# Retention layers of a four-layer decoder: value and gate columns as seven block products, queries and keys as eight

## The reference

```python
def retention_mixer(x, s0, pos, w_in, norm_g, w_out):
    q, k, v, g = jnp.split(x @ w_in, [hk, 2 * hk, 2 * hk + hv], axis=-1)   # 1024, 1024, 2048, 2048 columns
    q = rope(q.reshape(b, l, RET_HEADS, RET_KEY_DIM), pos)
    k = rope(k.reshape(b, l, RET_HEADS, RET_KEY_DIM), pos) * (RET_KEY_DIM ** -0.5)
    o, s_fin = retention_chunked(q, k, v, s0)                              # 4 heads, chunks of 128 rows
    o = layer_norm_without_gain(o) * norm_g
    y = (jax.nn.silu(g) * o) @ w_out
    return y, s_fin
# every layer: x <- LN(alpha*x + mixer(x)); x <- LN(alpha*x + (silu(x @ a) * (x @ u)) @ w_out)
```

## Time and profile before

| | |
|---|---|
| median of three runs | 3132.41 us (3131.67 to 3133.89) |
| the profiled execution | 3135.14 us, span of its profile 3133.5 us |
| TensorE busy | 2976.5 us, 95% of the span |
| VectorE busy | 2024.7 us, 65% |
| ScalarE busy | 1248.3 us, 40% |
| granted clock, mean over the span | 0.971 of full speed |
| first retention layer, one head in the steady part (193.2 to 321.9 us) | 128.7 us |

### The profile page before, as it was taken

How to read it: one execution, slowest core, us unless ns; L and a number is a source line. 1 busy time by engine, 2 the same in 40 slices (tenths; PEclk the granted TensorE clock), 3 DMA queues, 4 the chain that set the end, 5 groups by cost and what they waited for, 6 DMA issues and landing times.

```text
span 3133.5 us, 54106 instructions
## 1 busy us (share of the span) xinstructions
PE 2976.5 (95%) x22655; PEld 2798.6 (89%) x22655; DVE 2024.7 (65%) x3062; ACT 1248.3 (40%) x1881; POOL 209.2 (7%) x342
## 2 busy tenths in 40 slices
PE   7999998999996999998898899999999999899998
PEld 7898996899996999987798799999989989699998
DVE  4555554868577957767886485857555555585766
ACT  3332332535343634443343153534523333253543
POOL 0102111000000000011011100000021110100000
PEclk9999999999997999998998999999999999899999
DMA  6344443233331333332122323333343433323332
GB/s 154 128 126 158 128 138 115 79 102 103 95 88 41 87 96 101 97 97 59 48 75 87 123 68 102 102 95 101 96 157 120 157 129 112 128 75 99 105 99 63
DMA packets 492948, 323.77 MB, mean 103 GB/s; under 512 B 29723, under 2 KB 469275, under 8 KB 492698
## 3 DMA queue, kind: packets, MB, share of 16 engines
q1 hardware_dynamic: 465906, 230.14, 26.3%
q0 software_dynamic: 26800, 90.18, 8.2%
HBM read 275.90 MB, written 44.82 MB: 102 GB/s over the span
## 4 chain that ended last, share of the span: by engine, by line
PE 88%; DVE 6%; ACT 3%; issue 2%; DMA 0%; POOL 0%; DVEq 0%; SPq 0%; ACTq 0%; POOLq 0%
PE ps L522 46%; PE ps L2728 8%; PE ps L2730 8%; PE ps L2729 8%; PE ps L572 2%; PE ps L2223 2%; PE ps L573 2%; PE ps L574 2%; PE ps L553 2%; PE ps L2355 2%; PE ps L2345 1%; DVE wf L2137 1%; ACT w_h L493 1%; DVE wf L2185 1%; PE ps L2820 1%
## 5 line engine op out<-in xcount | busy, mean ns | idle before, releaser
L522 PE MATMUL ps<-rr,w_h 128*128 128x260 f32 x3968 | 638.4, 283 | 2.2 <-DVE w_l L499 1.1
L499 DVE TENSOR_TENSOR w_l<-w_raw,w_h 128x1024 fp32r<-128x1024 f32 (+2 forms) x312 | 336.7, 1079 | 391.8 <-ACT w_h L493 390.6
L522 PEld LDWEIGHTS ps<-rr,w_h 128*128 128x128 f32 x3968 | 544.0, 189 | 4.1 <-issue 3.0
L493 ACT ACTIVATE w_h<-w_raw 128x1024 fp32r<-128x1024 f32 (+2 forms) x312 | 293.4, 941 | 481.0 <-PE ps L522 443.4
L522 PE MATMUL ps<-x_h,w_h 128*128 128x260 f32 x2016 | 419.7, 290 | 9.0 <-DVE w_l L499 7.5
L522 PE MATMUL ps<-x_h,w_l 128*128 128x260 f32 x2016 | 407.9, 284 | 0.0
L522 PE MATMUL ps<-x_l,w_h 128*128 128x260 f32 x2016 | 407.7, 284 | 0.0
L522 PE MATMUL ps<-rr,w_l 128*128 128x260 f32 x1984 | 400.2, 283 | 0.0
L2728 PE MATMUL ps<-x_h,w_h 128*128 128x260 f32 x1280 | 362.5, 283 | 5.7 <-ACT wf L1229 5.7
L2729 PE MATMUL ps<-x_l,w_h 128*128 128x260 f32 x1280 | 361.5, 282 | 0.0
L2730 PE MATMUL ps<-x_h,w_l 128*128 128x260 f32 x1280 | 361.0, 282 | 0.0
(11 more groups left out here) (330 smaller groups left out, 5070.6 us busy)
## 6 DMA issues: line engine op xcount, KB each, us to landing
w_raw<-in_ffn_w_in SPq DMA_DIRECT2D x176, 512.0 KB, 4.1
w_raw<-in_ret_w_in SPq DMA_DIRECT2D x96, 512.0 KB, 3.9
out<-wf POOLq DMA_DIRECT2D x72, 512.0 KB, 3.3
wf<-in_state_ret POOLq DMA_DIRECT2D x64, 512.0 KB, 5.6
w_raw<-in_ffn_w_out SPq DMA_DIRECT2D x64, 512.0 KB, 4.3
w_raw<-in_ret_w_out SPq DMA_DIRECT2D x64, 256.0 KB, 2.8
w_raw<-in_dsa_w_in SPq DMA_DIRECT2D x27, 512.0 KB, 3.9
w_raw<-in_ffn_w_out SPq DMA_DIRECT2D x32, 384.0 KB, 4.0
```

Source lines behind the costliest of these rows:

```text
L493: C.activation(whole(stage, k, half_of(w_h, n)[:, 0:m]), landed(stage, k, n, m), ACT.Copy).then_inc(S["w_hi"], 1)
L499: V.tensor_tensor(whole(stage, k, half_of(w_l, n)[:, 0:m]), landed(stage, k, n, m), whole(stage, k, half_of(w_h, n)[:, 0:m].bitcast(F32)), ...
L522: mm = M.matmul(ps[:, 2 * (n % 2) + b, 0:HALF], lhs[:, c, :], rhs[:, c, cols], start=(c == 0 and term == 0), stop=(c == cs - 1 and term == 2))
```

## The change

1. **Values and gates.** The units (4,5), (6,7), (8,9), (10,11) of each head become pairs. A pair is two units by all 520 rows, cut into blocks of four chunks and 260 rows, and formed as seven products instead of eight: P1, P2, P5, P6, P7, P4, P3, of 12 matmuls each, 84 for a pair in place of 96. Four of the weight blocks are sums of quarters of `w_raw`, formed on VectorE (L616 of the new kernel, semaphore `tq`); the row blocks of P5, P6, P7 and P3 are sums of rows of `x`, formed once for each layer (`row_sum`, stage `pre`). On TensorE the order is P1, P2, P6, P5, P7, P4, P3. P1, P6, P7 and P4 go on adding into one PSUM bank, and ScalarE copies it out after each (`snap`, semaphore `pa`); P2 and P3/P5 have a bank each; VectorE combines three times (`pd`).
2. **Queries and keys** of heads 1 to 3 become three blocks, U1, U2, UD, of 24, 12 and 12 matmuls, 48 as before. Head 0's stay whole.
3. **Weights.** `w_h` and `w_l` are four blocks of 512 columns (a pair's product, or an output unit), split by `feed_hi` on ScalarE and `feed_lo` on VectorE four blocks ahead.
4. **Before a retention layer** VectorE forms the four row sums (1040 elements wide) and ScalarE and VectorE split them; the scaling of `x` by alpha on ScalarE (`xs`) stands behind three of the splits.
5. **Moved.** `keys`, `values(0)`, and on the other engines what prepares them: `rope(1)`, `qk_hi(1)`, `qk_lo(1)` stood before units 4 and 5, and now stand behind the pair (4,5); `keys` and `values(0)` stand behind `project`, before the pair (6,7).
6. **FFN.** The third group of a pair's summed weights (1536 columns) has its own tiles `e_h`, `e_l` and is split in one piece, without the separate piece `lone`; the split of the first output stage's unit 1 waits for the last P3.
7. **Other.** The mask of a head's scores is loaded by GpSimd after the gating of the head before; three loads of small constants move from SyncE to GpSimd; tiles are laid over one another anew.

The core of the diff (`-` before, `+` after):

```diff
+SPLIT_ORDER = ("P1", "P2", "P5", "P6", "P7", "P4", "P3")
+RUN_ORDER = ("P1", "P2", "P6", "P5", "P7", "P4", "P3")
...
+            V.tensor_tensor(ret_block(w_l, n), ret_raw(stage, n), ret_block(w_h, n).bitcast(F32), ALU.subtract
+                            ).then_inc(S["w_lo"], 1)
+            to, other = dict(P1=(0, 2), P2=(2, 3), P5=(0, 3), P6=(1, 0), U2=(0, 1))[name]
+            dve.wait_ge(*ret_mark("w_lo", stage, i, k, name))
+            if name == "P1":
+                dve.wait_ge(*arrived(stage, i, k + 1))
+            elif name != "U2":
+                dve.wait_ge(*at("tq", base + dict(P2=1, P5=2, P6=3)[name]))
+            V.tensor_tensor(quarter(stage, i, k, to), quarter(stage, i, k, to), quarter(stage, i, k, other), ALU.add
+                            ).then_inc(S["tq"], 1)
...
+                for j in (2, 1, 3):
+                    sum_hi(j)
+                act.wait_ge(*pre("ss", 4))
                 C.activation(x[:], x[:], ACT.Copy, scale=ALPHA).then_inc(S["xs"], 1)
...
+                        snap("P1", one[:, 0:HALF], k)
+                        feed()
+                        feed()
+                        snap("P6", two[:, 0:HALF], k + 1)
+                        feed()
+                        feed()
+                        for step in mid1:
+                            step()
+                        snap("P7", two[:, HALF:T], k + 1)
+                        feed()
+                        for step in mid2:
+                            step()
+                        act.wait_ge(*ret_mark("mm", stage, i, k, "P4"))
...
+                    pair(4)
+                    act.wait_ge(*at("head_in", 32))
+                    tail(5)
                     qk_hi(1)
...
-                    scale_state(i, 1)
-                    step(8, lambda: silu_g(0))
...
+                        feed()
+                        dve.wait_ge(*ret_mark("mm", stage, i, k, "P2"))
+                        combine(one[:, 0:HALF], 2, 1, ALU.add)
+                        feed()
+                        feed()
+                        feed()
+                        for step in mid1:
+                            step()
+                        combine(two[:, HALF:T], 3, 3, ALU.subtract)
+                        feed()
+                        for step in mid2:
+                            step()
+                        feed()
+                        dve.wait_ge(*ret_mark("mm", stage, i, k, "P3"))
+                        combine(two[:, 0:HALF], 3, 2, ALU.subtract)
+                        feed()
...
+                    pair(4, (), [lambda: tail(4)])
+                    dve.wait_ge(*at("head_in", 32))
+                    tail(5)
                     rope(1)
                     qk_lo(1)
-                    step(4)
-                    tail(4)
-                    dve.wait_ge(*at("head_in", 48))
-                    step(5)
-                    tail(5)
                     if i:
                         project(i - 1)
                     for t in range(QT):
...
+                    pair(10, [lambda: new_state(i, 1), lambda: stats(i, 2)],
+                         [lambda: stats(i, 3), lambda: centre(i, 2), lambda: centre(i, 3), lambda: new_state(i, 2)])
...
+                    pe.wait_ge(*at("pa", 4 * q + 1))
+                    if (i, k) == (0, 4):
+                        pe.wait_ge(*pre("ss_lo", 3))
+                    product(i, k, "P6", own, False)
+                    pe.wait_ge(*at("pd", 3 * q - 6))
+                    product(i, k, "P5", 3, True)
+                    for step in mid1:
+                        step()
+                    pe.wait_ge(*at("pa", 4 * q + 2))
+                    product(i, k, "P7", own, False)
+                    for step in mid2:
+                        step()
+                    pe.wait_ge(*at("pa", 4 * q + 3))
+                    product(i, k, "P4", own, False)
+                    pe.wait_ge(*at("pd", 3 * q - 4))
+                    if (i, k) == (0, 4):
+                        pe.wait_ge(*pre("ss_lo", 4))
+                    product(i, k, "P3", 3, False)
...
+                    pair(i, 4, (), [lambda: tail(4)])
                     if i:
                         turn_outputs(i - 1, 4, ("s_new", 2 * NB))
+                        project(i - 1)
                     keys(0)
                     keys(1)
                     values(0, ())
-                    if i:
-                        project(i - 1)
-                    unit(i, 6)
-                    values(1, ())
-                    scores(0, ("kn_lo", 2))
-                    scores(1, ("kn_lo", 4))
-                    unit(i, 7)
+                    pair(i, 6, [lambda: values(1, ()), lambda: scores(0, ("kn_lo", 2))], [lambda: scores(1, ("kn_lo", 4))])
...
+                    pair(i, 8, [lambda: values(3, ("att_m", 2))], [lambda: values(4, ("v_lo", 3))])
...
-                    unit(i, 11)
+                    pair(i, 10, [lambda: spread_v(i, 1), lambda: outputs(2, ("o_n", 1))],
+                         [lambda: outputs(3, ("o_n", 2)), lambda: spread_v(i, 2)])
                     spread_v(i, 3)
```

More of the change, by code:

```diff
@@ L660, in head_constants @@
                 def head_constants(i):
-                    pool.dma_start(mask, head(A["decay"], i)).then_inc(S["head_in"], 16)
                     pool.dma_start(hc(i, 0, 8), head(A["head_col"], i)).then_inc(S["head_in"], 16)
@@ L1396, in ret, with feed, row_sum, sum_lo @@
                     dve.wait_ge(*marks.here(stage)("rtab_in", 0))
+                fed, pre = iter(range(2, len(RET_EVENTS))), marks.here("pre" + stage[3:])
+                def feed():
+                    feed_lo(dve, stage, next(fed))
+                def row_sum(j, one, op, other):
+                    V.tensor_tensor(sr[:, j - 1], one, other, op).then_inc(S["ss"], 1)
+                def sum_lo(j, turn):
+                    dve.wait_ge(*pre("ss_hi", turn))
+                    V.tensor_tensor(ret_l[j - 1], sr[:, j - 1], ret_h[j - 1].bitcast(F32), ALU.subtract
+                                    ).then_inc(S["ss_lo"], 1)
@@ new lines, in ret, with product @@
+                pre = marks.here("pre" + stage[3:])
+                def product(i, k, name, bank, fresh):
+                    n = SPLIT_AT[i, k, name]
+                    pe.wait_ge(*ret_mark("w_lo", stage, i, k, name))
+                    wh, wl = (ret_block(w, n).rearrange("p (c n) -> p c n", n=P) for w in (w_h, w_l))
+                    hi, lo = rows[name]
+                    out = ps[:, bank, 0:HALF]
+                    for c in range(4):
+                        M.matmul(out, wh[:, c], hi[:, c], start=fresh and c == 0, stop=False, skip_group_check=True)
+                        M.matmul(out, wh[:, c], lo[:, c], start=False, stop=False, skip_group_check=True)
+                        mm = M.matmul(out, wl[:, c], hi[:, c], start=False, stop=c == 3, skip_group_check=True)
+                    mm.then_inc(S["mm"], 1)
@@ new lines, in pair @@
+                def pair(i, k, mid1=(), mid2=()):
+                    at, q = marks.here(stage, i), k // 2
+                    own = (6 * i + q) % 2
+                    pe.wait_ge(*at("pa", 8 if k == 4 else 4 * q - 4))
+                    if i and k == 6:
+                        pe.wait_ge(*marks.here(stage, i - 1)("z_add", 7))
+                    product(i, k, "P1", own, True)
+                    if i and k == 6:
+                        pe.wait_ge(*marks.here(stage, i - 1)("z_add", 8))
+                    pe.wait_ge(*at("pd", max(3 * q - 8, 0)))
+                    product(i, k, "P2", 2, True)
+                    pe.wait_ge(*at("pa", 4 * q + 1))
[16 more added lines that the diff above has]
+                    product(i, k, "P3", 3, False)
@@ new lines, in output @@
+                def output(i, k, halves_of=(0, 1)):
+                    n = SPLIT_AT[i, k, None]
+                    pe.wait_ge(*ret_mark("w_lo", stage, i, k, None))
+                    wh, wl = (ret_block(w, n).rearrange("p (c n) -> p c n", n=P) for w in (w_h, w_l))
+                    if len(halves_of) == 1:
+                        cols = prompt_halves()[halves_of[0]]
+                        for c in range(VC):
+                            mm = three(ps[:, 2 * (k % 2) + halves_of[0], 0:HALF], wh[:, c, :], wl[:, c, :],
+                                       gate_h[:, c, cols], gate_l[:, c, cols], c == 0, c == VC - 1)
+                    else:
+                        for c in range(VC):
+                            for lhs, rhs, term in ((wh, gate_h, 0), (wh, gate_l, 1), (wl, gate_h, 2)):
+                                for b, cols in enumerate(prompt_halves()):
+                                    mm = M.matmul(ps[:, 2 * (k % 2) + b, 0:HALF], lhs[:, c, :], rhs[:, c, cols],
+                                                  start=(c == 0 and term == 0), stop=(c == VC - 1 and term == 2))
+                    if halves_of[-1] == 1:
+                        mm.then_inc(S["mm"], 1)
@@ L2254, in unit, with block @@
```

(16 more changed lines are left out.)

440 lines of the change are left out of this document (265 added, 175 removed).

## The result

The changed kernel took 3149.23 us, median of four runs (3145.95 to 3153.69), against 3132.04 for the kernel before: 1.0059 times as long, 95% interval 1.0043 to 1.0075. Five more runs of it gave 3151.99 (3149.99 to 3156.03, ratio 1.0060, 1.0047 to 1.0074); 3151.99 is also the median of all nine. The forecast was 3151.

What follows compares the result with a forecast made beforehand. TensorE, busy all 128.70 us of a head, bounds the kernel, so every wait is lost. 66.2 us added less 47.8 removed, +18.4, gave 3153.5 on the profiled execution, hence 3151 forecast; range 3139 to 3163, 8-in-10 range 3115 to 3174.

Steps and rivals of the forecast that it cites:

- Matmuls removed: 32 pairs in the retention layers with 12 matmuls fewer each: 384 at 0.120 us, 46.1 us less.
- FFN start: TensorE's 1.07 us wait for a `snap` at the FFN's start shrinks by 0.4 in each of four layers, 1.7 us.
- Rotation ahead of the first addition: Heads 1 to 3: VectorE's key rotation delays `z_add`, so unit 14 waits about 2.4 us, six times, 14.4 us.
- P4 of pair (8,9): P4 waits for ScalarE's third `snap` behind other ScalarE work: 1.2 us, eight times, 9.6 us.
- Last `spread_v`: Behind pair (10,11) it waits for VectorE's `new_state(2)`, behind statistics and two `centre`s: 0.85 us, eight times, 6.8 us.
- Head 0: `keys` wait 7.0 us for the rotation, and P1, P6, P4 wait within the first pair: 10.8 us, twice, 21.6.
- Second layer's start: Row sums and high parts precede ScalarE's scaling of `x` in the second retention layer: unit 2 comes 5.4 us later.
- Clock: Half clock behind long waits: 2.75 us for each wait before `keys`, 1.1 at the second layer's start, 6.6 in all.
- the first (smooth pairs, 3122): Pairs run as smoothly as in the FFN, idle under 0.3 us before P4 of (8,9): 3122 us, chance 0.27.
- The second: Every wait of 2 us or more, at unit 14 and before P6, drops the clock: 22 us lost, 3173, chance 0.07.
- The third: VectorE or the weights late at more places, 0.8 us in each of 24 pairs: 19 us, 3170, chance 0.16.
- the fourth: Terms nearly cancel: head 0's `keys` wait 4 us, waits within pairs half as long: 3132, no difference, chance 0.12.

Runs made afterwards that it cites:

- The experiment: Changed kernel with only `scale_state(1)` on ScalarE moved behind the third `snap` in the pair (8,9): 3143.74 us, ratio 1.0042.
- all four edits: Changed kernel with rotation spread over projection (heads 1 to 3), `scale_state(1)` behind third `snap`, head 0's rotation behind second combination, `x` scaled later: 3117.67 us, ratio 0.9957.

## Why the prediction was right

The direction, the time and the mechanism held: fewer matmuls, and more waits of TensorE than they were worth. Step by step:

- **Matmuls removed**: 384, as counted. TensorE's busy time fell by 36.0, not by 46.1; in a head at full clock about 1 us is left over that I did not foresee, and no run tried why. Rows at the seams of products account for part of it: the changed kernel's timeline has, behind four transposes, the first matmul of a product 0.21 ahead of the second, where others are 0.12 apart,

```profile
353.57 0.60 PE L2411 MATMUL ps<-ident,rf 128*128 128x128 f32 x4
353.92 0.37 PE L2439 MATMUL ps<-sr_h,w_h 128*128 128x260 f32 x1
354.13 0.28 PE L2440 MATMUL ps<-sr_l,w_h 128*128 128x260 f32 x1
354.24 0.28 PE L2441 MATMUL ps<-sr_h,w_l 128*128 128x260 f32 x1
```

  and the change cuts a head's input units into 15 pieces, where there were 12. Over the pieces, the starts beyond an even 0.119 us come to 1.9 us in a head before and 2.4 in the changed kernel, waits left out: about half of the 1 us. The rest stays open.
- **FFN start**: 0.4 a layer was too much; in the first layer the wait fell from 1.07 to 0.93.
- **Rotation ahead of the first addition**: 2.4 forecast, 1.91 to 1.94 measured, six times, ended by VectorE's addition. Moving the rotation removed it.
- **P4 of pair (8,9)**: 1.2 forecast, 1.24 measured, eight times. The experiment showed that `scale_state` made it.
- **Last `spread_v`**: 0.85 forecast, 0.51 measured, and the order of `new_state` and `centre` was the cause.
- **Start of pair (4,5), heads 1 to 3**: 0.3 forecast, no wait in the trace.
- **Head 0**: 7.0 forecast for `keys` and 6.98 measured; within the pair 0.9, 2.1 and 0.75 forecast and 0.75, 1.95 and 0.48 measured.
- **Second layer's start**: 5.4 forecast, 8.50 - 3.21 = 5.3 measured. The scaling's place, to which I gave all of it, explained 2.5; the low parts of the row sums, which I did not list, stood behind it.
- **Clock**: the two waits before `keys` were followed by 2.3 and 2.0 us lost (5.51 at 0.58 and 0.64) where I had 2.75. The clock behind waits of 1.9 I costed at nothing; behind four or five of six 1.7 each was lost.

The waits in the sum came to 59.6 and measured 51.1. This error of 8.5 was made good by a term that the sum did not have, the 8 us of busy time. Of the clock, the two profiles together show this: summed over stretches of 2 us, the busy time of TensorE that half clock cost was 1.6 us in the heads of the retention layers before and 13.4 after, but 71.4 and 61.1 everywhere else. So the heads lost more than the 6.6 of the sum, the rest of the program lost less, which nobody forecast, and the net is 1.6. The closeness of 3151 owes something to luck. In the profiled execution the account is 51.1 of waits, 8 of busy time and 1.6 of clock, less 46.1, and less about 3.6 of small gains at the layers' ends and in the FFN: 11.0; its span rose by 10.2.

Of the rivals, the first (smooth pairs, 3122) was decided at the place it named: P4 waited 1.24, not under 0.3. With that place alone mended the time was 3143.74, and with all four edits 3117.67. The second, that each wait of 2 us drops the clock, happened in part: behind four of the six waits at unit 14, at 1.7 instead of 2.75, and behind neither of the two before P6 (granted clock 1.00 from 57.35 to 62.35, and the same in the second layer). The section of the Trainium skill named there ("TensorE: Matmul & The Clock Gate", "A second HAM failure mode: psum-queue depth-cycling") agrees with this trace in kind: brief idle times in dense work were followed by a lower clock, at 185 and 442 us, but not at 314. The third, more waits from a full VectorE, did not happen: at 77% of a head, or 98 us of work, no wait was left in a head from head 1 on beyond 0.21 once the order was mended. Nor did the fourth: `keys` waited 6.98, not 4, and P4 1.24, not half of 1.2.

## What to carry to other kernels

Count what a removed matmul gives, then walk each engine's list at the new places and ask which step stands between TensorE and the buffer it waits for; here moving a few steps, with all work kept, turned 0.6% slower into 0.7% faster. An engine's busy share said nothing of this: VectorE had the same 98 us a head in both versions. When a stage is to run beside another, spread its operations over the idle times which that stage leaves, rather than putting them in one piece ahead of its first short step.
